# A 64-byte pad below the large SBUF buffers of a three-layer fp32 network kernel

## The reference

```python
h = h + mixer(rmsnorm(h, g1))            # layer 0: HGRN2; layer 1: dilated attention; layer 2: RG-LRU and gated convolutions
gate, up = split(rmsnorm(h, g2) @ w_in)  # [512,1024] @ [1024, 2*2816]
h = h + (silu(gate) * up) @ w_down       # [512,2816] @ [2816,1024]
```

## Time and profile before

| | |
|---|---|
| device time, median of 3 | 2096.45 us |
| the profiled execution's own time | 2095.66 us |
| span of its instructions | 2093.9 us |
| PE busy in the span | 2084.9 us (100%) |
| PE weight loads (beside PE) | 1736.5 us (83%) |
| DVE / ACT / POOL busy | 1039.8 / 741.0 / 1142.3 us |
| mean granted TensorE clock | 0.999 of 2.4 GHz |
| chain that ended last | 98% PE |

### The profile page before, as it was taken

The page is one execution under the profiler, slowest core; times in us unless marked ns, Lnnn a source line. Parts: engine busy times, 40 slices in busy tenths (PEclk is TensorE's granted clock), DMA queues, the critical chain, the costliest instruction groups (busy, mean ns, idle before and its releaser), DMA issues.

```text
span 2093.9 us, 28284 instructions
## 1 busy us (share of the span) xinstructions
PE 2084.9 (100%) x11203; PEld 1736.5 (83%) x11203; DVE 1039.8 (50%) x1224; ACT 741.0 (35%) x866; POOL 1142.3 (55%) x822
## 2 busy tenths in 40 slices
PE   9999999999999999999999999999999999999998
PEld 7888888888888889888888888888888888888887
DVE  6487654555113356634555333744477544553226
ACT  6336532212224455443122233515433332222244
POOL 6677555555455433365555555544566555555553
PEclk9999999999999999999999999999999999999999
DMA  5222132222333222242222232322222222223321
GB/s 199 82 66 78 49 113 100 100 87 94 105 116 105 86 80 82 81 141 100 90 90 100 100 102 100 103 96 101 100 87 94 101 100 100 96 86 108 120 100 62
DMA packets 33211, 204.41 MB, mean 98 GB/s; under 512 B 3688, under 2 KB 6504, under 8 KB 9456
## 3 DMA queue, kind: packets, MB, share of 16 engines
q1 hardware_dynamic: 32896, 203.13, 28.3%
q10 hardware_dynamic: 240, 0.23, 0.0%
HBM read 200.19 MB, written 2.10 MB: 97 GB/s over the span
## 4 chain that ended last, share of the span: by engine, by line
PE 98%; DVE 0%; DMA 0%; ACT 0%; SPq 0%; issue 0%; DVEq 0%; ACTq 0%
PE bank L2103 98%; DMA first_raw<-wall 0%; DVE x L1977 0%; PE bank L2490 0%; PE bank L2381 0%; PE bank L2517 0%; SPq L630 0%; ACT w_hi L828 0%; DVE h L2079 0%; PE bank L2492 0%; ACT un L828 0%; PE bank L2242 0%; ACT rr L828 0%; DVE ao_lo L1909 0%; ACT first_whi L828 0%
## 5 line engine op out<-in xcount | busy, mean ns | idle before, releaser
L688 POOL TENSOR_TENSOR w_lo<-raw,w_hi 128x512 fp32r<-128x512 f32 x676 | 976.6, 1475 | 857.6 <-ACT w_hi L828 857.6
L2103 PE MATMUL bank<-u_hi,w_hi 128*128 128x512 f32 (+1 forms) x1936 | 752.5, 389 | 0.1
L2103 PE MATMUL bank<-u_lo,w_hi 128*128 128x512 f32 (+1 forms) x1936 | 749.5, 387 | 0.0
L828 ACT ACTIVATE w_hi<-raw 128x2048 fp32r<-128x2048 f32 x185 | 354.2, 1915 | 914.4 <-PE bank L2103 911.3
L2103 PE MATMUL bank<-u_hi,w_lo 128*128 128x512 f32 (+1 forms) x1936 | 482.1, 387 | 0.0
L2103 PEld LDWEIGHTS bank<-u_hi,w_hi 128*128 128x128 f32 x1936 | 363.6, 188 | 74.4 <-ACTq L1249 0.5
L2103 PEld LDWEIGHTS bank<-u_lo,w_hi 128*128 128x128 f32 x1936 | 363.7, 188 | 73.6
L2103 PEld LDWEIGHTS bank<-u_hi,w_lo 128*128 128x128 f32 x1936 | 362.5, 188 | 74.5
L2103 PE MATMUL bank<-act_hi,w_hi 128*128 128x512 f32 x528 | 205.4, 389 | 0.0
L2103 PE MATMUL bank<-act_lo,w_hi 128*128 128x512 f32 x528 | 205.4, 389 | 0.0
L1390 DVE TENSOR_TENSOR h<-h,bank 128x512 f32<-128x512 f32 x48 | 30.8, 683 | 300.6 <-PE bank L2103 300.6
(11 more groups left out here) (306 smaller groups left out, 2127.0 us busy)
## 6 DMA issues: line engine op xcount, KB each, us to landing
raw<-wall SPq DMA_DIRECT2D x185, 1024.0 KB, 4.9
out_t<-h SPq DMA_DIRECT2D x8, 256.0 KB, 2.8
h<-x_t SPq DMA_DIRECT2D x3, 512.0 KB, 6.8
first_raw<-wall SPq DMA_DIRECT2D x6, 256.0 KB, 7.1
av_moved<-av SPq DMA_DIRECT2D x14, 64.0 KB, 2.1
h<-x_t SPq DMA_DIRECT2D x2, 256.0 KB, 3.8
first_raw<-wall SPq DMA_DIRECT2D x4, 128.0 KB, 3.9
lmask_f<-lmask_in SPq DMA_DIRECT2D x1, 512.0 KB
```

The lines of the kernel that those rows point to most:

```text
L688: ins = nc.gpsimd.tensor_tensor(w_lo[:, s, c], raw[:, s, c], w_hi[:, s, c].bitcast(F32), ALU.subtract)
L828: return nc.scalar.activation(out, in_, func, **k)
L2103: return nc.tensor.matmul(out, lhsT, rhs, start=start, stop=stop, skip_group_check=True)
```

## The change

The pad in front of the two regions is 32 floats per partition in place of 16, so 128 bytes in place of 64. `region_u` then starts at 106432 and `region_a` at 139200, both 64 bytes past a multiple of 128, and region a ends at 229312, 64 bytes under 224 KiB (229376). All that is allocated in front of the pad stays where it was. No instruction, wait, size or order changes; only the addresses of operands in the two regions do.

```diff
-        sb("pad", [P, 16])
+        sb("pad", [P, 32])
         region["u"] = (nc.sbuf_base + 31) // 32 * 32
         sb("region_u", [P, 2 * KC * S])
         region["a"] = (nc.sbuf_base + 31) // 32 * 32
         sb("region_a", [P, 2 * FT * S])
```

## The result

The changed kernel takes 2137.98 us (median of 4 runs, 2137.70 to 2138.19) against 2096.4 us before (median of 4): ratio 1.02, 95% interval 1.0188 to 1.0213. The forecast was 2096.4 us with a range up to 2104, so it was wrong by 41.6 us.

What follows compares the result with a forecast made beforehand. The prediction took PE's stream of matmuls at a fixed 226.7 ns cadence as the bound; 2093.9 us of span plus four terms of 0, 2095.7 with 1.8 around it, forecast as the median 2096.4 us, range 2091 to 2104.

Steps and rivals of the forecast that it cites:

- the frame: Whole kernel: one stream of PE matmuls at a fixed cadence; time moves only if the cadence, start or end does.
- the small terms: Start 0.3 us longer, or a few strided weight loads 3 ns longer, 0.7 us; together 2097.4 us, counted as the same.
- the arithmetic of the stake: Matmul stream: 8160 moving reads from the two regions, at 226.7 ns 1850 us, 88% of the span; any cost multiplies uncovered.
- the sign that was named for being wrong: L2103 records in 1500 to 1900 us stay within two of 1766; a cadence moving over 0.5 ns means wrong.
- a pair of streams 64 bytes apart is neither faster nor slower there. Price 0: Moving against stationary operand: from `fac` against `sel_r`, 230 ns each like the neighbours in front, a cost of 0.
- The row that the 8160 moving reads were priced by: Product with `ones_r` as both operands, 32 bytes past a multiple of 128: 111.8 ns against 112.0, taken as no difference.
- 0 (8160 moving reads): 512-column matmuls reading moving operands from the two regions: 0 us, between outer ends of +68 and -109 us.
- The slower rival: Matmul stream: moving reads off the 128-byte grid cost one to four cycles each, 3.4 to 13.6 us; chance 0.10.
- My argument against it: Matmul stream: the same 32-cycle surplus at 512 and 256 columns shows no toll by bytes; 226.7 holds across different operands.
- The faster rival: Matmul stream: moving reads and weight loads clash at the same grid place, 64 bytes apart they miss; up to 109 us; chance 0.04.
- outer bound of +68 us: Matmul stream: the slowest 512-column cadence, strided weight slices at 235.0 ns, 8.3 ns over, times 8160.

Runs made afterwards that it cites:

- experiment 7: Three benches of matmuls alone on constant data, not the kernel, with varied entries, stops, widths and types; at distance 64 228.9 ns, or 233.3 in 6 of 16 segments.
- experiment 1: All buffers, weights included, 64 bytes higher than in the kernel before, by a pad in front of `h`: 2096.64 us, ratio 1.0003.
- the bench: Matmuls alone on constant data, other engines idle, operands shifted by varied bytes, not the kernel: 226.6 ns at distance 0, 229.1 at 64, 233.2 at 192.

## Why the prediction was wrong

Right were the frame and the small terms: PE alone sets the time, no new wait, weight loads within 1 ns, VectorE's groups within 2 ns, the start +0.15 us against bounds of 0 and 0.3. Right was also the arithmetic of the stake, 8160 matmuls without cover. And the sign that was named for being wrong came: 1733 records in 1500 to 1900 us where 1766, within two, were forecast.

The step that failed is "a pair of streams 64 bytes apart is neither faster nor slower there. Price 0". It rested on the earlier trace rows, where two matmuls with `sel_r` took 230 ns each, and compared them with neighbours at 230. Those neighbours were slow for a reason of their own, strided weight slices. `fac` stands at 128 and `sel_r` at 64 modulo 256, distance 64, and against the kernel's undisturbed 226.7 the pair was slow: 3.3 ns each by the rounded rows, 4.8 by the records' nanoseconds (232 and 231), and 3.3 to 4.3 in the four other such pairs of the trace. Times 8160 that is 27 to 39 us. Two matmuls at a break in the stream cannot separate the relation from the break, so the nearness to the 41.6 us measured is partly luck; but the only row of the trace that had the new relation spoke for a loss, and I read it as nothing.

The row that the 8160 moving reads were priced by, the product with `ones_r` in the earlier trace rows, could not show the loss either. Both of its operands are the same tensor, so its distance is 0 wherever the tensor lies, and it is plain fp32, the type that experiment 7 found indifferent to the distance (429 ns at 0, 64 and 192). The term "0 (8160 moving reads)" was in truth +39.9 us of the 42.2, and 2.4 us more came from the 480 matmuls of `by_tokens`, where the weights move and `u` stands still.

The slower rival had the right place and sign but the wrong mechanism and size. It was a toll on an address off the 128-byte grid, of one to four cycles; experiment 1 shows that such an address costs nothing if the weights stand there too. The real term is 16 cycles of 2.4 GHz (6.67 ns) in one state and 2.2 ns in the other. My argument against it, that the surplus was the same 32 cycles at 256 and 512 columns, only showed distance 0 twice. The faster rival named the relation of the two streams, and was right in that, with the sign reversed: 0 is the good place. The range had an upper end of 2104 because I let the nearest row outweigh an outer bound of +68 us; for a mechanism with no cover and no row at that place, the bound belonged in it.

What stays open: why two reads interact at all, why by 256 bytes, why in steps such as 16 cycles, why a shift of both by an odd multiple of 16 costs, and why fewer weight columns don't help. No run here shows the inside of it.

## What to carry to other kernels

When back-to-back float32r matmuls with a weight load each set the time, keep moving and stationary operands at a distance of 0 modulo 256 bytes for 512 columns and 128 weight columns, both on multiples of 32 bytes, and measure the distance for other widths; a stray small allocation in front of a large buffer can cost 2%. Read the cadence from starts, by stage, and compare a foreign row with the undisturbed cadence, not with its neighbours. A change of layout alone can move a constant such as `ones_r` and with it the time of all that follows, so an edit that shifts addresses needs this look before its own effect is judged.

## What the runs showed of the hardware that was not expected

- The cadence of float32r matmuls depends on the two operands' addresses modulo 256 bytes: 226.7 ns at 0, 228.9 at 64, 233.3 at 192, up to 239.7 at 244; 230.0 at 0 with both operands 16 bytes off. Bf16 (215.8 ns) and plain fp32 (429 ns per record) don't show it in the distances tried.
- It has states that last: over 1500 matmuls at 233.3 in one. At distance 64 a single foreign matmul chooses, by where its weights lie and on which of the stream's three steps it falls (6 of 6 that fell on one step locked, 0 of 10 of the others), and one program varied from 2122 to 2140 us between runs.
- The Trainium skill, "SBUF — State Buffer", section "Who interferes with whom", calls TensorE's two read ports independent, one for the moving operand and one for the weight load. For bf16 the bench agrees, 215.8 ns at four distances. For float32r the measurement does not look so: 226.7 or 233.3 by the place of the weights alone, with no other engine at work. That the ports themselves are where the two meet is not shown.
